# A one-core decoder step: the last chunk's route, and an embedding product spread over the first three experts

## What is computed

```python
def moe(xf, w_router, b_router, w1, b1, w2, b2):          # top 4 of 32 experts
    logits = xf.astype(F32) @ w_router.astype(F32) + b_router.astype(F32)
    top_v, top_e = lax.top_k(logits, TOP_K)
    gates = jax.nn.softmax(top_v, axis=-1)
    ...
    def run_block(args):
        e, toks, g = args
        xb = xf[toks]
        h = xb @ w1[e] + b1[e]                            # 1024 x 2048
        glu = jnp.minimum(h[:, ::2], SWIGLU_LIMIT)
        lin = jnp.clip(h[:, 1::2], -SWIGLU_LIMIT, SWIGLU_LIMIT)
        a = glu * jax.nn.sigmoid(SWIGLU_ALPHA * glu) * (lin + 1)
        out = a @ w2[e] + b2[e]                           # 1024 x 1024
        return out * g[:, None].astype(out.dtype)
...
    y = x2 + jax.nn.sigmoid(x2 @ w_ple_gate) * (p.astype(x2.dtype) @ w_ple)
```

## Time and profile before

| what | us |
|---|---|
| median of 3 runs | 1109.31 |
| the profiled execution | 1109.61 |
| its span, first to last instruction | 1107.8 |
| PE busy / DVE busy / ACT busy / POOL busy | 1075.3 / 437.3 / 159.4 / 78.9 |
| first expert product on PE | 151.42 |
| bytes moved by DMA | 440.63 MB, 398 GB/s on average |

### The profile page before, as it was taken

The page is one execution under the profiler, slowest core; times in us unless marked ns, Lnnn a source line. Parts: engine busy times, 40 slices in busy tenths (PEclk is TensorE's granted clock), DMA queues, the critical chain, the costliest instruction groups (busy, mean ns, idle before and its releaser), DMA issues.

```text
span 1107.8 us, 15186 instructions
## 1 busy us (share of the span) xinstructions
PE 1075.3 (97%) x5608; PEld 428.8 (39%) x5608; DVE 437.3 (39%) x1109; ACT 159.4 (14%) x306; POOL 78.9 (7%) x107
## 2 busy tenths in 40 slices
PE   9999999999999999999999999999999999999998
PEld 7786433333333333333333333333333333333334
DVE  1648663333333333333333333333333333332245
ACT  1532341000000000000000000000000000000033
POOL 0747420000000000000000000000000000000000
PEclk9999999999999999999999999999999999999999
DMA  9979999999999999999999999999999999999961
GB/s 317 269 308 399 294 361 393 430 426 427 428 431 428 427 429 429 428 427 431 428 427 428 429 429 427 430 429 428 427 429 428 427 426 429 427 426 429 426 259 40
DMA packets 52624, 440.63 MB, mean 398 GB/s; under 512 B 10560, under 2 KB 17980, under 8 KB 27397
## 3 DMA queue, kind: packets, MB, share of 16 engines
q1 hardware_dynamic: 51545, 439.00, 95.8%
q0 software_dynamic: 368, 0.57, 0.2%
q10 hardware_dynamic: 676, 0.59, 0.2%
HBM read 436.61 MB, written 3.77 MB: 398 GB/s over the span
## 4 chain that ended last, share of the span: by engine, by line
PE 58%; DMA 23%; DVE 9%; SPq 5%; issue 2%; POOL 1%; ACT 1%; DVEq 0%; POOLq 0%
PE bank L999 25%; DMA ring<-in_w_mlp 22%; PE bank L1070 16%; PE bank L958 4%; DVE proj L1629 3%; PE bank L1150 3%; PE bank L778 3%; DVE proj L1626 2%; DVE proj L1624 2%; PE bank L1051 1%; SPq L378 1%; PE bank L971 1%; POOL ring L2107 1%; PE bank L993 1%; PE bank L1059 1%
## 5 line engine op out<-in xcount | busy, mean ns | idle before, releaser
L999 PE MATMUL bank<-ring,proj 128*64 128x512 f32 x2024 | 460.9, 597 | 14.1 <-DMA ring<-in_w_mlp 13.4
L1590 DVE SCALAR_TENSOR_TENSOR xT<-bank,proj,xT 128x512 f32<-128x512 f32 x128 | 90.2, 747 | 423.7 <-PE bank L958 422.4
L999 PEld LDWEIGHTS bank<-ring,proj 128*64 128x64 f32 x2024 | 140.6, 136 | 290.0 <-issue 261.9
L1070 PE MATMUL bank<-ring,pool_side 128*64 128x512 f32 x1024 | 226.8, 595 | 0.4 <-ACT pool_side L1963 0.4
L1070 PEld LDWEIGHTS bank<-ring,pool_side 128*64 128x64 f32 x1024 | 71.3, 137 | 133.5 <-issue 129.1
L1957 ACT ACTIVATE proj<-proj 128x256 f32<-128x256 f32 x64 | 26.7, 417 | 546.1 <-DVE proj L1623 545.1
L1581 DVE TENSOR_SCALAR proj<-bank,ln_rows_of_pairs 128x64 f32<-128x64 f32 x256 | 67.5, 337 | 24.5 <-PE bank L971 24.5
L958 PE MATMUL bank<-mixT 64*128 64x512 f32 x264 | 74.5, 641 | 0.9 <-ACT mixT L1966 0.5
L599 PE MATMUL bank<-xT,ring 128*128 128x264 f32 x320 | 74.3, 388 | 0.2 <-ACT proj L1776 0.2
L599 PEld LDWEIGHTS bank<-xT,ring 128*128 128x128 f32 x320 | 60.0, 190 | 12.3 <-issue 1.6
L937 PE MATMUL bank<-xreg,proj 128*64 128x512 f32 x248 | 58.7, 592 | 0.0
(11 more groups left out here) (369 smaller groups left out, 632.6 us busy)
## 6 DMA issues: line engine op xcount, KB each, us to landing
ring<-in_w_mlp SPq DMA_DIRECT2D x190, 2048.0 KB, 29.4
ring<-in_w_in SPq DMA_DIRECT2D x9, 1024.0 KB, 14.4
ring<-in_w_out SPq DMA_DIRECT2D x4, 1024.0 KB, 9.5
ring<-in_w_ple_gate SPq DMA_DIRECT2D x4, 1024.0 KB, 29.3
xreg<-in_x_prompt SPq DMA_DIRECT2D x4, 512.0 KB, 4.7
ring<-q_row SPq DMA_DIRECT2D x1, 2048.0 KB, 7.3
ring<-k_row SPq DMA_DIRECT2D x1, 2048.0 KB, 7.0
out<-ring SPq DMA_DIRECT2D x1, 2048.0 KB, 15.7
```

The costliest lines, as they stand in the source:

```text
L999: last = pe.matmul(bank[q][BLOCK * t:BLOCK * (t + 1), :], xgT[:, k % 4, k // 4, :], rows_[:, col:col + 512], start=False, stop=(k == KD - 1))
L1070: last = pe.matmul(bank[4][BLOCK * h:BLOCK * (h + 1), :], aT[:, m, BLOCK * t:BLOCK * (t + 1)], w[:, k % 2, 512 * h:512 * h + 512], start=F ...
L1590: ins = STT(total[:, c, s], ins_bank[h][:, :], gate_table[:, c, bass.ds(n, 1)], total[:, c, s], ALU.mult, ALU.add)
```

## The change

Three things move.

- On PE the counts of chunks 0 and 2 (EARLY_PLACES) now stand ahead of turn_quarter, and the counts in bank 3 ahead of router, of chunk 1.
- The early embedding products leave the way to expert 0: the two halves of chunk 1 stand in experts 0 and 1 (a piece behind k = 1 and one behind k = 3), the samples' in expert 2 behind k = 5. They use banks 2, 3 and 5, so PE waits in each of these experts for ACT's copy (ple_done) before the next gather. The first four experts are written out ahead of the loop on PE and ACT. The turned embedding rows (early_pT) and the gate rows share a new place, gate_space.
- The load of late[1] moves from ahead of pair 1 to behind pair 16 (n = 46) on SP, since its place now holds the embedding weights until expert 2.

```diff
--- before.py
+++ after.py
@@ -177,7 +177,9 @@
         ROW_G, ROW_EMT, ROW_WK, ROW_SC = 0, 2, 4, 6
         maxdiag = [xreg[32 * c:32 * c + HEADS, 2056 + 512 * c:2568 + 512 * c].rearrange("p (h t) -> p h t", h=HEADS)
                    for c in range(2)]
-        gates = sb("gates", [2 * HEADS, TOK])
+        gate_space = sb("gate_space", [P, 2 * (P + SAMPLES)])
+        gates = gate_space[0:2 * HEADS, 0:TOK]
+        early_pT = gate_space[:, :].rearrange("p (k n) -> p k n", k=2)
         gcol = small[:, 0:28]
         dec_b = small[:, 28:32]
         nout = small[0:HEADS, 36:37]
@@ -261,7 +263,6 @@
         logit_parts = part(P + SAMPLES + P)
         LOGIT_PARTS = {0: logit_parts[:, 0:P], 2: logit_parts[:, P:P + SAMPLES], 1: logit_parts[:, P + SAMPLES:]}
         places = part(3 * 2 * EXPERTS).rearrange("p (c r e) -> p c r e", c=3, r=2)
-        early_pT = part(2 * (P + SAMPLES)).rearrange("p (k n) -> p k n", k=2)
         assert off[0] <= TILES * TOK
         off[0] = routing_at
         glu = part(256)
@@ -340,7 +341,7 @@
         QUARTERS = (bank[7], bank[6])
         EARLY_PLACES = bank[4][:, 256:256 + 2 * EXPERTS]
         P_BANK = bank[1][:, 0:2 * P]
-        EMBED_BANKS = {0: (bank[1], bank[6]), 1: (bank[4], bank[7]), 2: (bank[5],)}
+        EMBED_BANKS = {0: (bank[1], bank[6]), 1: (bank[2], bank[3]), 2: (bank[5],)}
         GATE_BANKS = {0: (bank[5][:, :], bank[0][:, :]), 2: (bank[1][:, 0:256],),
                       1: (bank[5][:, :], bank[0][:, 0:256], bank[2][:, 0:256])}
         PIECES = {0: (slice(0, 512), slice(512, 1024)), 1: (slice(0, 512), slice(512, 768), slice(768, 1024))}
@@ -479,11 +480,12 @@
             load_next(6)
             sp.wait_ge(sem("mix_ps"), 5)
             load_next(14)
-            sp.wait_ge(sem("ple_ps"), 3)
-            load_late(1)
             for n in range(SLOTS, UNITS * STEP, 2):
                 sp.wait_ge(sem("units_used"), n - SLOTS + 2)
                 load_next(n)
+                if n == SLOTS + 30:
+                    sp.wait_ge(sem("ple_ps"), 3)
+                    load_late(1)
 
             def load_body(e, done, closing=0):
 
@@ -865,9 +867,6 @@
             turn_rows(1, 0, 4)
             logit_rows(1)
             mix(1, second, range(6, KD), (1,))
-            turn_quarter(0)
-            turn_quarter(1)
-            router(1, 6)
 
             def early_embedding(half, ks):
 
@@ -911,19 +910,19 @@
             pe.matmul(EARLY_PLACES[:, EXPERTS:2 * EXPERTS], ones16, mask[:, 0, :], start=False, stop=False)
             pe.matmul(EARLY_PLACES[:, EXPERTS:2 * EXPERTS], before16[0:SAMPLES, :], mask[0:SAMPLES, 2, :],
                       start=False, stop=True).then_inc(sem("pos_ps"), 1)
+            turn_quarter(0)
+            turn_quarter(1)
             pe.matmul(bank[3][:, 0:3 * EXPERTS], ones16[0:1, :], far_row, start=True, stop=False)
             count_places(0, (1,))
             count_places(2, (1,))
+            router(1, 6)
             logit_rows(2)
-            pe.wait_ge(sem("ple_in"), 16)
-            early_samples()
             pe.wait_ge(sem("ln1_ready"), 4)
             pe.wait_ge(sem("onehot_ready"), 1)
             gather_chunk(0)
             gather_chunk(2)
             pe.wait_ge(sem("mask_ready"), 3)
             count_places(1, ()).then_inc(sem("pos_ps"), 1)
-            early_embedding(0, (0,))
 
 
             def gather(n):
@@ -981,7 +980,7 @@
                     missing = 1 if closing and s == slot_of(0) else 0
                     pe.wait_ge(sem(f"slot{s}"), i4 * 12 + 16 * (before[s] + landings(u) - missing))
 
-            def expert(n, j, closing=0):
+            def expert(n, j, closing=0, opening=False):
 
                 i4 = n - j
                 final_one = closing == 2 and j == STEP - 1
@@ -1024,6 +1023,8 @@
                         for back in (1, 0):
                             product(k - back, ring[:, s - back, :], 1).then_inc(sem("units_used"), 1)
 
+                    if opening and j < 2 and k in (1, 3):
+                        early_embedding(j, (k // 2,))
                     if k == 1:
                         pe.wait_ge(sem("out_done"), n + 1)
                         pe.wait_ge(sem("comb_read"), n * 3 + 1)
@@ -1033,7 +1034,12 @@
                         combine(1, (j + 1) % 2)
                     elif k == 5:
                         combine(2, (j + 1) % 2)
-
+                        if opening and j == 2:
+                            pe.wait_ge(sem("hotT_done"), 3)
+                            early_samples()
+
+                if opening and j < 3:
+                    pe.wait_ge(sem("ple_done"), j + 1)
                 if not final_one:
                     if j == 0:
                         pe.wait_ge(sem("sample_moved"), 7)
@@ -1078,16 +1084,16 @@
             turn_places()
             pe.wait_ge(sem("xg_copied"), 1)
             turn_gathered()
-            early_embedding(0, (1,))
-            early_embedding(1, (0, 1))
             pe.wait_ge(sem("places_split"), 1)
-            pe.wait_ge(sem("ple_done"), 1)
             pe.wait_ge(sem("onehot_ready"), 3)
             spread_places(0)
             pe.wait_ge(sem("ln1_in"), 48)
             pe.wait_ge(sem("passes_ready"), 1)
             npass = pe.value_load(extra[0:1, 0:1], min_val=0, max_val=PASSES - 1) + 1
-            with pe.Fori(0, npass * EXPERTS - 2 * STEP, STEP) as n:
+            pe.wait_ge(sem("ple_in"), 16)
+            for j in range(STEP):
+                expert(j, j, opening=True)
+            with pe.Fori(STEP, npass * EXPERTS - 2 * STEP, STEP) as n:
                 for j in range(STEP):
                     expert(n + j, j)
             for closing in (1, 2):
@@ -1668,7 +1674,6 @@
             hot_turned(0, 0)
             dve.wait_ge(sem("ln1_in"), 16)
             begin_sum(total[:, 0, :], 0, "total_ready")
-            dve.wait_ge(sem("ple_ps"), 3)
             dve.wait_ge(sem("dve_chain"), counts["dve_chain"])
             for q in range(4):
                 groups = [a.rearrange("b (h q j) -> b q h j", h=2, q=4)[:, q] for a in (xtok[0:SAMPLES, 2, :], ln1_row[0:SAMPLES, :])]
@@ -1941,12 +1946,9 @@
             parts_out(2)
             ln1_rows(2, 1, 6)
 
-            act.wait_ge(sem("ple_ps"), 1)
-            act.copy(embedded_samples, EMBED_BANKS[2][0][:, 0:256]).then_inc(sem("ple_done"), 1)
-
             def embedded_early(half):
 
-                act.wait_ge(sem("ple_ps"), half + 2)
+                act.wait_ge(sem("ple_ps"), half + 1)
                 act.copy(embedded_rows[:, 512 * half:512 * half + 512], EMBED_BANKS[1][half][:, :]).then_inc(sem("ple_done"), 1)
 
 
@@ -1968,19 +1970,15 @@
             act.wait_ge(sem("gathered"), 1)
             act.copy(hist_mix[:, 0:512], bank[2][:, :]).then_inc(sem("xg_copied"), 1)
             warm = stat[:, 57:58]
-            embedded_early(0)
+            act.nop().then_inc(sem("out_done"), 1)
             for i in range(3):
                 top_exp(i)
             act.activation(warm, eps, ACT.Sigmoid)
-            embedded_early(1)
-            act.wait_ge(sem("ple_done"), 3)
-            act.nop().then_inc(sem("out_done"), 1)
             act.wait_ge(sem("gates_table"), 2)
             for q in range(1, 4):
                 act.copy(gate_table[32 * q:32 * q + SAMPLES, 2, :], gate_table[0:SAMPLES, 2, :])\
                    .then_inc(sem("sample_moved"), 1)
             act.wait_ge(sem("sample_begun"), 4)
-            act.wait_ge(sem("ple_ps"), 3)
             act.copy(part_high, xtok[0:SAMPLES, 2, :]).then_inc(sem("part_cast"), 1)
             for q in range(1, 3):
                 act.copy(pos_table[32 * q:32 * q + SAMPLES, 2, :], pos_table[0:SAMPLES, 2, :])\
@@ -1994,7 +1992,14 @@
             act.wait_ge(sem("sample_moved"), 7)
             act.wait_ge(sem("passes_ready"), 1)
             npass = act.value_load(extra[0:1, 0:1], min_val=0, max_val=PASSES - 1) + 1
-            with act.Fori(0, npass * EXPERTS - STEP, STEP) as n:
+            for j in range(STEP):
+                if j < 2:
+                    embedded_early(j)
+                elif j == 2:
+                    act.wait_ge(sem("ple_ps"), 3)
+                    act.copy(embedded_samples, EMBED_BANKS[2][0][:, 0:256]).then_inc(sem("ple_done"), 1)
+                expert(j, j)
+            with act.Fori(STEP, npass * EXPERTS - STEP, STEP) as n:
                 for j in range(STEP):
                     expert(n + j, j)
             for j in range(STEP):
```

## The result

The changed kernel takes 1112.74 us (median of 9 runs, 1111.03 to 1116.8), the kernel before 1109.1 (9 runs beside it): a ratio of 1.0039, 95% interval 1.0027 to 1.005. It is slower, by 3.6 us between the medians, where the forecast was +0.65 us and no difference; the time lies just above the predicted range.

What follows compares the result with a forecast made beforehand. The weight stream's bytes at 428 GB/s, from where it becomes unbroken, were taken to set the end. Terms -2.5 + 2.45 + 0.5 + 0.2 = +0.65 us gave a median of 1110.0 us, range 1107.4 to 1112.6.

Steps and rivals of the forecast that it cites:

- earlier start, with the shallow queue: Start of the weight stream: pairs asked for earlier gain 2.5 us; a shallow queue at pairs 8 to 10 costs 0.5.
- late[1] in the stream: Spare unit loaded behind pair 16, in the unbroken weight stream: its 1.05 MB cost 2.45 us (bounds 0 and 2.7).
- more code: First four experts written out on PE and ACT: loading code costs 0 to 0.3 us of stream, taken as 0.2.
- rows turned: Last chunk's route and gather before expert 0: DVE starts the turned rows 1.2 us sooner (bounds 0.65 and 2.16).
- first product: PE's first expert product, behind the route, starts near 148.3 us, 3.1 us sooner.
- pair 1 at 152.13: SP asks for the first pair of units that refills the weight ring at about 152.0 us.
- x: End of expert 0, and pair 5's request with it, comes 0.7 us sooner (bounds -0.6 and 1.2).
- Pair 5's landing: Weight pair 5 meets an empty queue and lands 7.6 us after its issue, at 183.3, 2.9 us sooner.
- What a lead is worth: Bytes behind the point where the weight stream becomes unbroken, at 428 GB/s, set the end; gain there 2.5 us.
- The one with 1112.7: Weight pairs 8 to 11 land 23.5 us for four, pair 11 later than about 215.3; +3.4 us; chance 0.20.
- PE's start in full: End follows PE's 3.1 us earlier start if the spare unit finds room in the stream: 1106.2 us; chance 0.13.
- The route came sooner: Before expert 0; its rival said no sooner, another chain holding the gather: 1110.6 to 1111.2 us, chance 0.14.

Runs made afterwards that it cites:

- e11: Kernel before with counts first, embedding products left out, ACT copying a constant instead, fillers as in e1; spare unit and loops unchanged: 1107.99 us, ratio 0.9984.
- e1: Changed kernel with six filler products on constants, results unread, on PE between the steps of the route: 1111.2 us, ratio 1.0015.
- e2: e1 without the load of late[1]; the unit of expert 24 reads late[0] instead, so outputs differ: 1108.95 us, ratio 0.999.
- e3: Kernel before with late[1] loaded behind pair 16, as in the changed kernel: 1111.54 us, ratio 1.0023.
- e12: e11 with the first four experts written out ahead of the loops on PE and ACT as well: 1108.7 us, ratio 0.9994.
- e9: Kernel before with the first four experts written out ahead of the loops on PE and ACT, nothing else: 1110.65 us, ratio 1.0011.
- e6: e1 with POOL's two 4 KB ln2 loads issued early, at about 131 us: 1110.69 us, ratio 1.0014.
- e8: Changed kernel with two fillers of 256 columns only where the samples' embedding stood: 1112.28 us, ratio 1.0029.
- e4: Changed kernel with the turn and the router back ahead of the counts: 1115.58 us, ratio 1.0047.
- e10: Kernel before with the counts first, ahead of the last chunk's turn and router, nothing else: 1108.9 us, ratio 0.9995.

## Why the prediction was wrong

| step of the sum | predicted | measured | from |
|---|---|---|---|
| earlier start, with the shallow queue | -2.5 + 0.5 | -1.6 | e11 |
| late[1] in the stream | +2.45 | +2.25, +2.48 | e1 less e2; e3 |
| more code | +0.2 | +0.7, +0.9 to 1.1 | e12 less e11; e9 |
| clock of the route | none | +1.5 | changed kernel less e1 |
| sum | +0.65 | +2.9 to +3.5 | +3.6 measured |

The measured terms are differences of medians, each uncertain by about a microsecond, and the clock's by more, since the runs of the changed kernel lie in groups; that they nearly add up is a check, not a proof. The embedding products inside the experts have no row of their own.

- **The step that failed first is one that was not there.** The working read "the TensorE clock at full" from 200 to 300 us and worked out the route with durations at that clock as well; the clock there fell to 0.50. It counted the embedding products as 4.9 us of PE work that leaves, and never asked what they do for the clock while PE waits for DVE and ACT. At 0.994 this costs 3.5 to 5.4 us against the median of the runs at 1.000, at 1.000 nothing: the three such runs, median 1111.4, are e1's time.
- **Up to expert 0 the steps held, once the clock did** (e1): rows turned 1.3 us sooner (1.2), first product 148.46 (148.3), pair 1 at 152.13 (152.0), x = 1.07 (0.7, up to 1.2). By pair 5's issue x is 0.7 in e6, 0.2 in e2 and -0.1 in e8, so 0.7 was on the high side but within its bounds.
- **Pair 5's landing held, except in e1's profile.** It was put at 7.6 us after its issue, as on an empty queue. It took 8.1 in the changed kernel, 8.0 in e2 and e8, 7.7 in e6, and 10.3 in e1.
- **What a lead is worth was right.** Bytes at 428 GB/s behind the start of the unbroken stream were taken to carry every microsecond to the end. In the six kernels with the loops as before they do, to within 0.4 us.
- **The small costs were mis-sized.** Code was priced as bytes over 16 engines, 0 to 0.3 us, taken at 0.2, and the embedding in the experts at nothing beyond 0.4 us in expert 1. From pair 6 to the last pair, against the kernel before, the stream takes 0.4 and 1.3 us longer with the code (e9, e12), and 1.5 to 2.1 us with the code and the embedding. By the times, e9 and e12 give 0.7 to 1.1, not clear of noise. That a block holds up one engine and not a sixteenth of all fits these sizes, but isn't shown.
- **late[1] was right**, in size and in mechanism: 14.0 us to landing, 2.5 us of the stream, no wait behind it.
- **The rivals.** The one with 1112.7 has nearly the measured time, but not its mechanism: pairs 8 to 11 of the changed kernel land 4.9 to 5.3 us apart, not 5.9. Pair 11 does land later than the 215.3 that was to decide for it, at 217.76, but pair 5 was already 1.8 us late, by the clock. PE's start in full falls with e2, where it starts 2.1 us sooner and gains nothing. The route came sooner once the clock held, as e1 shows.

What stays open: whether a block falls on one engine, and which blocks cost time; how much of the loss in the stream is code and how much the embedding in the experts; and what exactly makes the clock fall. No rule for that follows from these rows: from 136 to 141 us the changed kernel has more PE work than before (4.37 us against 3.93) and e4 the same 3.93, e9 has the same work up to 142, and yet the clock falls in all three profiles and not in that of the kernel before.

## What to carry over

Work on TensorE that seems to be in the way between short dependent steps may be what keeps its clock up, as here (from 142 to 154 us 1.00 in the kernel before, 0.50 without the embedding products, 1.00 with the fillers of e1, and yet 0.86 in e9, which keeps them): before taking it out, look at how idle the engine gets there, and hold the place with filler products to see what the change is worth at the same clock. Beside a weight stream that runs without a gap, price every byte that joins it at the stream's rate: the spare unit's 1.05 MB came to 2.25 and 2.48 us, where 428 GB/s gives 2.45. Blocks of code may cost more than that: with five more of 16 KB, an estimated 0.2 us at 428 GB/s, the stream took 0.4 and 1.3 us longer than before (e9, e12). An earlier start was worth here what it gave the first pair of the unbroken stream, and that reached the end (e11: 1.7 us sooner at pair 6, 2.0 at the last pair): read the lead there, and measure it alone, without the rest of the change.

## What was not expected of the hardware

- The granted clock differs from run to run of the same kernel. Runs with a mean under 0.998 were 6 of 9 of the changed kernel, 6 of 6 of e4, 2 of 12 of e8, 1 of 11 of e9, none of 11 of e1 or e10, and 1 of the 35 of the kernel before that stand beside e8. In the profiled execution of the changed kernel, mean 0.994, the fall is one short stretch: 1.00 up to 141 us, 0.51 from 141 to 154, 0.99 from there to 200 and 1.00 behind.
- One packet of code, 16 KB, takes about 1.1 us of an engine's time in a stream of 428 GB/s. Most packets delay no pair of weights that the landings show; the kernels with five more of them lose 0.4 to 2.1 us in the stream.
- In e1's profile four packets of a 4 KB load took 2.0 us of engine time beside the weights; in the changed kernel, from 177 to 186 us, all 32 packets of such a load took 1.0%, 1.4 us. The pair of weights under way landed 10.3 us after its issue in the one and 8.1 in the other.
